# The first pair of MLP-up tiles by eight plain products in the second half of a layer norm, in front of 31 pairs by seven products

## The reference, cut to what matters

```python
h = layer_norm(ALPHA * x + mix, ln1_g, ln1_b)          # (576, 2048)
f = square(relu(einsum('btd,df->btf', h, w_mlp1)))      # w_mlp1 (2048, 8192)
y = layer_norm(ALPHA * h + einsum('btf,fd->btd', f, w_mlp2), ln2_g, ln2_b)
```

## Time and profile before

| | us |
|---|---|
| median of 3 runs | 2711.6 (2711.41 to 2714.79) |
| the profiled execution: its time | 2708.59 |
| its span, first to last instruction | 2706.8 |
| mean granted TensorE clock | 0.986 of full speed |
| PE busy | 2593.7 |
| DVE busy | 2004.7 |
| ACT busy | 1073.2 |

### The profile page before, as it was taken

One profiled execution on the slowest core, in us unless ns is written; L12 is line 12 of the kernel. 1 busy time (PEld: TensorE's weight loads), 2 busy tenths in 40 slices (PEclk: granted clock), 3 DMA queues, 4 the chain that ended last, 5 costly groups with the idle time before them and its releaser, 6 DMA issues.

```text
span 2706.8 us, 51737 instructions
## 1 busy us (share of the span) xinstructions
PE 2593.7 (96%) x20061; PEld 2477.8 (92%) x20061; DVE 2004.7 (74%) x3181; ACT 1073.2 (40%) x1361; POOL 70.3 (3%) x118
## 2 busy tenths in 40 slices
PE   8999999998889999987999999999999999999998
PEld 8999999995657777887999999999999999999997
DVE  5788732326875555689888888888888888888898
ACT  3111111115874444455555555555433333333333
POOL 1000000000000100000000000000000000000001
PEclk9999999998999999998999999999999999999998
DMA  8776643316026775754555555555795556555642
GB/s 260 231 240 207 191 85 79 79 49 237 2 71 213 246 247 176 213 158 138 187 185 187 190 189 188 185 185 185 277 313 181 185 177 211 184 182 180 194 126 86
DMA packets 514888, 480.20 MB, mean 177 GB/s; under 512 B 49276, under 2 KB 465300, under 8 KB 503862
## 3 DMA queue, kind: packets, MB, share of 16 engines
q1 hardware_dynamic: 509722, 411.57, 48.7%
q0 software_dynamic: 4736, 67.18, 6.6%
q10 hardware_dynamic: 332, 0.11, 0.0%
HBM read 387.89 MB, written 99.16 MB: 180 GB/s over the span
## 4 chain that ended last, share of the span: by engine, by line
PE 64%; DVE 6%; ACT 3%; issue 2%; DMA 1%; SPq 1%; DVEq 0%; ACTq 0%
PE ps L2619 50%; PE ps L2535 3%; PE ps L2462 3%; PE ps L2440 2%; PE ps L2330 1%; PE ps L2400 1%; PE ps L2384 1%; PE ps L2320 1%; DVE pS L1574 1%; PE ps L2344 1%; DMA f_b<-f_scratch 1%; PE ps L2416 1%; DVE w_sl L1774 0%; ACT sS L1000 0%; ACT pT L962 0%
## 5 line engine op out<-in xcount | busy, mean ns | idle before, releaser
L1128 ACT ACTIVATE w_sh<-w_s 128x1024 fp32r<-128x1024 f32 (+1 forms) x512 | 473.6, 949 | 783.3 <-PE ps L2619 522.6
L2619 PE MATMUL ps<-f_b,w_sh 128*128 128x288 f32 x3584 | 713.8, 295 | 8.4 <-DMA f_b<-f_scratch 6.0
L1774 DVE TENSOR_TENSOR w_sl<-w_s,w_sh 128x1024 fp32r<-128x1024 f32 (+1 forms) x512 | 554.3, 1088 | 123.9 <-ACT w_sh L1128 123.5
L2619 PEld LDWEIGHTS ps<-f_b,w_sh 128*128 128x128 f32 x3584 | 574.3, 189 | 11.0 <-DMA f_b<-f_scratch 7.0
L2619 PE MATMUL ps<-f_b,w_sl 128*128 128x288 f32 x1792 | 527.1, 294 | 0.0
L2619 PE MATMUL ps<-h_u,w_sh 128*128 128x288 f32 x2560 | 514.3, 296 | 11.4 <-DVE h_u L1909 10.9
L2619 PEld LDWEIGHTS ps<-h_u,w_sh 128*128 128x128 f32 x2560 | 411.1, 189 | 12.9 <-issue 6.8
L2619 PE MATMUL ps<-h_u,w_sl 128*128 128x288 f32 x1280 | 376.6, 294 | 0.0
L2619 PEld LDWEIGHTS ps<-f_b,w_sl 128*128 128x128 f32 x1792 | 338.9, 189 | 0.0
L861 ACT ACTIVATE w_hi<-w_raw 128x2048 fp32r<-128x2048 f32 x61 | 116.9, 1916 | 484.9 <-PE ps L2171 466.3
L2171 PE MATMUL ps<-x_hi,w_hi 128*128 128x288 f32 x1408 | 302.7, 297 | 0.0
(11 more groups left out here) (322 smaller groups left out, 3340.3 us busy)
## 6 DMA issues: line engine op xcount, KB each, us to landing
w_s<-in_w_mlp SPq DMA_DIRECT2D x512, 256.0 KB, 3.7
f_scratch<-f_st SPq DMA_DIRECT2D x32, 2016.0 KB, 9.0
f_b<-f_scratch SPq DMA_DIRECT2D x56, 1152.0 KB, 8.0
w_raw<-in_w_in SPq DMA_DIRECT2D x90, 512.0 KB, 5.1
e_raw<-in_w_out SPq DMA_DIRECT2D x16, 512.0 KB, 4.3
e_raw<-in_w_out SPq DMA_DIRECT2D x64, 128.0 KB, 3.3
wb<-in_cache_win SPq DMA_DIRECT2D x8, 1024.0 KB
w_raw<-in_w_out SPq DMA_DIRECT2D x64, 128.0 KB, 2.9
```

The lines of the kernel that those rows point to most:

```text
L1128: nc.scalar.activation(w_sh[m][:, :, :], blocks, ACT.Copy).then_inc(z_h[m], 1)
L1774: nc.vector.tensor_tensor(w_sl[m][:, :, :], blocks, w_sh[m][:, :, :].bitcast(F32), ALU.subtract).then_inc(z_l[m], 1)
L2619: last = nc.tensor.matmul(ps[:, bank, 0:TH], w[b][:, at_, cols], acts(k, x), start=(start and n == 0), stop=(stop and n == 2), skip_group_ ...
```

## The change

Pair 0 is computed by eight plain products: no block sums, neither of weights nor of activations. Two output tiles, two token halves, 8 steps of two input tiles, three matmuls each: 96 matmuls on the first token half and 96 on the second. Only the other 31 pairs (`KS`) go by seven products, so the loops run one turn fewer, and the structure that pair 0 had in the kernel before (`first_half_pair`, `up_half(0, 1)`) is now pair 1's.

- Weights: ACT copies both units whole (`std_high`, 128x2048), DVE subtracts (`std_low`: unit 0 in one piece, unit 1 in two).
- PE (`std_pair`): products of steps 0 to 3 on the first token half with the mean after the first, the 16 squares, steps 4 to 7 of tile 0, the spread, steps 4 to 7 of tile 1, then the second token half step by step as `h_u` comes.
- Activations: per step j only the two blocks of the second token half are split (`d_high`, `d_low`, 288 elements each); these two loops carry the shifts and scales. The old loop of sums and splits follows them, without shifts and scales; of the split only the wide one of the four sums is left (`h_high`, `h_low`), and the weight splits `low_12`, `low_56`, `low_22` of unit 0 stand behind its step 0.
- Result: ACT takes relu and square from PSUM into `f_std`, SP stores it to `g_scratch`, and when the last `h_low` is done loads it into `f_raw`. From there it goes the way of the others: `f_sums(-1)` is the first thing in DVE's up loop, `f_high(-1)` and `f_low(-1)` come in the second half of the next pair, then `f_store(-1)`.
- SP also issues the two units of the next pair between the units of pair 0 and the stores.

```diff
-NU = 2 * KP
+KS = KP - 1
+NU = 2 * KS
...
+            sp.wait_ge(s_lo, S_MLP + 1)
+            w_blocks(w1_v, 0, STD, 0)
+            sp.wait_ge(s_lo, S_MLP + 3)
+            w_blocks(w1_v, 1, STD, 1)
             for j in range(MP):
...
+            sp.wait_ge(s_acc, 4 + S_MLP)
+            sp.dma_start(g_dram[:, :, :], f_std[:, :, :]).then_inc(y_sv[0], 16)
             up_load(1, 0)
+            sp.wait_ge(y_sv[0], 64)
+            sp.wait_ge(y_sv[1], 80)
+            sp.wait_ge(h_lo_, 4 * MP)
+            sp.dma_start(f_raw[:, 0:4, :], g_dram[:, :, :]).then_inc(y_sv[0], 16)
             up_load(1, 1)
+            f_store(-1)
...
+            std_high(0)
+            std_high(1)
...
             for j in range(MP):
-                h_high(j)
+                d_high(j)
                 if j < MP - 2:
                     shift(2 * j + 4, 1)
                     shift(2 * j + 5, 1)
+            high_14(0, 0, 64)
+            act.wait_ge(s_gemm, 3 + S_MLP)
+            nc.scalar.activation(f_std[:, 0:3, :], banks(1, 3, TH), ACT.Relu)
+            nc.scalar.activation(f_std[:, 3, :], ps[:, 6, 0:TH], ACT.Relu).then_inc(s_acc, 1)
+            act.wait_ge(s_acc, 3 + S_MLP)
+            nc.scalar.activation(f_std[:, :, :], f_std[:, :, :], ACT.Square).then_inc(s_acc, 1)
+            for j in range(MP):
+                h_high(j)
+                if j == 0:
+                    high_12(0, 0)
+                    high_56(0)
+                    high_22(0, 0, 64)
...
-            unit_act(1, 1, 64, lambda: keep_1(0))
-            with act.Fori(1, KP) as i:
+            unit_act(1, 1, 64, lambda: (f_high(-1), keep_1(0)))
+            with act.Fori(1, KS) as i:
...
             for i in range(KT):
-                if i == KT - 1:
-                    sum_1(0, 0, 64)
-                    sum_23(0, 0)
-                    low_14(0, 0)
-                    sum_4(0, 0)
                 residual(S_OUT + i % XR, i, i % XR, 1, i // XR)
                 add_up(S_OUT + i, i, 1)
...
+                if i == KT - 2:
+                    std_low(0, 0, 4)
...
-            low_12(0, 0)
             dve.wait_ge(l_mean, 2)
             for k in range(KT):
                 subtract(k, 1)
-            low_56(0)
-            low_22(0, 0)
+            std_low(1, 0, 2)
             variance(1)
             invert(1)
+            std_low(1, 2, 4)
             dve.wait_ge(l_sd, 4)
             for k in range(4):
                 scale_1(k, 1)
             for j in range(MP):
-                h_sums(j)
                 if j < MP - 2:
                     scale_1(2 * j + 4, 1)
                     scale_1(2 * j + 5, 1)
+                d_low(j)
+            sum_1(0, 0, 64)
+            sum_23(0, 0)
+            low_14(0, 0)
+            for j in range(MP):
+                h_sums(j)
+                if j == 0:
+                    sum_4(0, 0)
                 h_low(j)
+                if j == 0:
+                    low_12(0, 0)
+                    low_56(0)
+                    low_22(0, 0)
...
-            second_half(0, before=False)
-            with dve.Fori(1, KP) as i:
+            f_sums(-1)
+            second_half(0)
+            with dve.Fori(1, KS) as i:
...
+            def std_pair():
+
+                pe.wait_ge(h_lo_, MP)
+                pe.wait_ge(s_lo, S_MLP + 1)
+                for j in range(CK):
+                    for n in range(2):
+                        std_part(n, j, 0)
+                    if j == 0:
+                        mean_half(1)
+                for k in range(KT):
+                    squares_half(k, 1)
+                for n in range(2):
+                    pe.wait_ge(s_lo, S_MLP + 2 + n)
+                    for j in range(CK, MP):
+                        std_part(n, j, 0)
+                    if n == 0:
+                        rep_half(1)
+                for j in range(MP):
+                    pe.wait_ge(h_lo_, MP + 2 * j + 2)
+                    for n in range(2):
+                        last = std_part(n, j, 1)
+                last.then_inc(s_gemm, 1)
...
+            std_pair()
             first_half_pair()
             up_half(0, 1, first=True)
-            with pe.Fori(1, KP) as i:
+            with pe.Fori(1, KS) as i:
```

More of the change, by code:

```diff
@@ L76 @@
 NSTEP = NCH * MP
-NU = 2 * KP
+KS = KP - 1
+NU = 2 * KS
+STD = 1
+Z0 = 64
 WC = CK * P
@@ L1108, in high_a, with std_high @@
                 nc.scalar.activation(h_a[:, j, :, 0, :], blocks_of(j)[:, 0:3:2, :], ACT.Copy).then_inc(h_hi_, 1)
+            def std_high(h):
+                act.wait_ge(z_raw[h], 64)
+                if h:
+                    act.wait_ge(s_gemm, 2 + S_MLP)
+                nc.scalar.activation(d_hi[h][:, :, :], w_s[:, RAW_AT[h]:RAW_AT[h] + 4, :], ACT.Copy).then_inc(s_hi, 1)
             nc.scalar.activation(pt_f[:, 0:1], w_of[:, 0:1], ACT.Sqrt)
@@ L1901, in h_sums, with d_low @@
                 nc.vector.tensor_tensor(raw[:, 4, :], view[:, 2, :], raw[:, 2, :], ALU.subtract).then_inc(h_t3, 1)
+            def d_low(j):
+                for n, (row, b) in enumerate(((0, 3), (3, 1))):
+                    dve.wait_ge(h_hi_, MP + 2 * j + n + 1)
+                    nc.vector.tensor_tensor(h_u[:, j // CK, row, j % CK, 1, :], blocks_of(j)[:, b, :], h_u[:, j // CK, row, j % CK, 0, :].bitcast(F32),
+                                            ALU.subtract).then_inc(h_lo_, 1)
             def h_low(j):
-                dve.wait_ge(h_hi_, MP + 2 * j + 1)
-                nc.vector.tensor_tensor(h_u[:, j // CK, 0, j % CK, 1, :], blocks_of(j)[:, 3, :], h_u[:, j // CK, 0, j % CK, 0, :].bitcast(F32), ALU.subtract).then_inc(h_lo_, 1)
-                dve.wait_ge(h_hi_, MP + 2 * j + 2)
+                dve.wait_ge(h_hi_, 3 * MP + j + 1)
                 dve.wait_ge(h_t3, 3 * j + 3)
@@ L2044, in step_dve @@
                 if opening:
-                    close_7(KP - 1)
+                    close_7(KS - 1)
                 low_12(t, u)
@@ L2104, in _ @@
                 if q == 0:
-                    f_sums(KP - 1)
+                    f_sums(KS - 1)
                 if q == 2:
-                    f_low(KP - 1)
+                    f_low(KS - 1)
             chunk_dve(1, after_first=True)
@@ L2640, in up_product, with std_part @@
                 product(m, UP_BANK[m], h_block(m, h), h == 0, h == 1, ready)
+            def std_part(n, j, half):
+                bank = (2, 3)[n] if half == 0 else (1, 6)[n]
+                h, cols = j // CK, slice(j % CK * P, (j % CK + 1) * P)
+                for a in range(2):
+                    hi, lo = d_hi[h][:, 2 * n + a, cols], d_lo[h][:, 2 * n + a, cols]
+                    x = [h_a[:, j, a, v, :] if half == 0 else h_u[:, h, (3, 0)[a], j % CK, v, :] for v in range(2)]
+                    for m, (w, v) in enumerate(((hi, x[0]), (hi, x[1]), (lo, x[0]))):
+                        last = nc.tensor.matmul(ps[:, bank, 0:TH], w, v, start=(j == 0 and a == 0 and m == 0),
+                                                stop=(j == MP - 1 and a == 1 and m == 2))
+                return last
+            def std_pair():
[4 more added lines that the diff above has]
+                        std_part(n, j, 0)
+                    if j == 0:
+                        mean_half(1)
[12 more added lines that the diff above has]
+                last.then_inc(s_gemm, 1)
             def first_half_pair():
                 pe.wait_ge(s_acc, 2 + S_MLP)
-                mean_half(1)
-                pe.wait_ge(h_lo_, MP)
                 pe.wait_ge(z_l[M1], 1)
                 up_product(M1, 0)
+                pe.wait_ge(s_acc, 3 + S_MLP)
                 pe.wait_ge(z_l[M2], 1)
                 up_product(M2, 0)
-                for k in range(KT):
-                    squares_half(k, 1)
-                rep_half(1)
                 pe.wait_ge(z_l[M3], 1)
@@ L2675, in up_half @@
                     pe.wait_ge(u_v, i)
-                up_product(M5, h, MP + 2 * CK + 2 if first else None)
+                up_product(M5, h, 3 * MP + CK + 1 if first else None)
                 if not first:
```

76 lines of the change are left out of this document (42 added, 34 removed).

## The result

The changed kernel takes 2719.04 us (median of 15 runs, 2715.77 to 2723.18) against 2711.60 us before (15 runs, 2707.96 to 2715.64): ratio 1.0025, 95% interval 1.0018 to 1.0032: **slower**, by a quarter of a per cent. The forecast was 2719.0 in 2712 to 2725.

The account below looks back on a forecast made before the run. The prediction took the norm's second half to be a chain of DVE and ACT, not matmuls. It summed 18.2 + 2.9 + 6.6 - 22.2 = +5.5, with the clock +7.4, on 2711.6 to 2719.0 us; range 2712 to 2725.

Parts of the forecast that it names:

- The frame: Whole change: one loop turn fewer, -22.2 us, against a later first loop turn; everything behind it costed at nothing.
- Step 1: Before the spread: 24 plain matmuls between squares and spread delay all scales and shifts by +1.2 us.
- Step 2: Plain second half: period 1.8 us, three sums now in the open; first `h_sums` starts +18.2 us later.
- PE hides entirely: Plain second half: PE ends near 1229.5; ACT's relu and square end before its first wide copy is due.
- Step 3: Old loop of sums and splits: a chain, no gain from removed work; added unit-0 low parts cost +2.9 us.
- The rival of a shrinking loop: Steps 1 to 7 of the old loop: period could fall to 3.0 us, 8.4 us less, 2710.6; chance 8%.
- Step 4: Last `h_low` to next pair: load, sums and splits in the open, 14.3 us instead of 7.7, +6.6 us.
- Step 5: Clock: PE's 4.5 us wait before the next pair's M1 drops it to half speed, +1.9 us (bounds 0 and 2.3).
- The sum: Whole kernel: +5.5 us, with the clock +7.4 us, giving 2719.0 us on the median, slower.
- about 3 us more: Sign on the profile page: PE busy about 3 us more, from 24 matmuls.

Follow-up runs that it names:

- experiment 1: Changed kernel with DVE making the block sums of step j+1 before the wide subtraction of step j: 2708.99 us, ratio 0.9986.
- experiment 2: Changed kernel with SP loading the plain result as soon as the block sums of step 6 are done: 2717.26 us, ratio 1.0018.
- experiment 5: Changed kernel with the plain result loaded twice in sequence, DVE and ACT waiting for the second load: 2723.03 us, ratio 1.0041.
- experiment 4: Changed kernel with 28 more matmuls, results unread, on PE ahead of the first loop turn: 2719.71 us, ratio 1.0027.
- experiment 8: Changed kernel with sums ahead, early result load, result's way behind the next unit's work, and spread before the 24 plain products: 2704.98 us, ratio 0.9977.
- second pair of profiles: Both kernels run again unedited: before 2712.34 us, ratio 1.0001; changed 2721.18 us, ratio 1.0031.
- experiment 3: Changed kernel with PE spreading the inverse root before the 24 plain products of tile 0's steps 4 to 7: 2722.36 us, ratio 1.0036.
- experiment 6: Changed kernel with the plain result's sums and split put behind the next unit's work, load unmoved: 2717.41 us, ratio 1.0018.
- experiment 7: Kernel before, with block sums of step j+1 ahead of the low parts of step j: 2710.64 us, ratio 0.9998.

## Why the prediction was right

- **The frame** (one pair fewer, -22.2 us, against a later first turn) held: MLP turns of 22.2 us behind the first. From the second turn's M1 to the end the two kernels take 1404.3 and 1406.1 us before, 1407.5 and 1405.1 us after, so single executions differ there by more than the kernels do.
- **Step 1.** The spread was forecast 14.1 us after the projection's last matmul and came at 14.7 (1216.00 - 1201.29), 1.8 later than before and not 1.2. Part of that is the step's own sum: its terms, 0.7 for the squares and 3.2 in place of 2.47, make +1.4 and not +1.2. The rest is size: the squares ended 1.0 us later, and from their end to the spread it took 3.3 us. The variance came some 0.4 us later too, but did not set the place: the inverse root was ready at 1214.46, and PE has no wait between the projection and 1219.9. So the 36 early products were not quite free either, as the step says. The removed unit-0 sums cost nothing: DVE still waits 1.43 us for PE before the last residual.
- **Step 2.** Periods of 1.71 us in place of 1.8 gave back what the spread lost: first `h_sums` at 33.5 us from the projection, forecast 33.8. "PE hides entirely" was not quite right: ACT's relu starts when PE ends, at 33.4 us from the projection and not 32.4 to 32.7, and with the square it held up ACT's first wide copy by some 0.4 us, which step 2 had taken for nothing.
- **Step 3** was the argument that mattered, and held: 4.24 us per step without scales and shifts, read off the last steps of the old loop. The low parts that the step adds took 2.87 us (1239.43 to 1242.30), forecast 2.9. What follows the wide subtraction of step 7 starts 74.5 us from the projection (1275.79 - 1201.29), forecast 74.3 (1250.35 + 18.2 + 2.9 - 1197.14). The rival of a shrinking loop fell, but its price was right: asked for by order (experiment 1), the period went to 2.93 us and the kernel lost 10 us.
- **Step 4.** 14.2 us from the last wide subtraction to the first turn, forecast 14.3; the load 3.5 us, forecast 3.7. Experiments 2 and 5 show from both sides that it sets the path: taken off it gives 2.7 us, doubled it costs 3.5.
- **Step 5.** The clock fell as taken, for 1.7 us (forecast 1.9), in both profiles of the changed kernel and not where the wait was filled (experiments 4 and 8). The premise that waits of about 2 us leave it up held for those two kernels' profiles and not in general (below).
- **The sum** was +7.4 us; the stage shows +7.2 and +7.4, the medians +7.4 and +8.0. That the agreement of the first median is to 0.04 us is chance: its parts missed by up to 0.65 us each, in both directions. One sign was missed: PE busy "about 3 us more" counted the 24 matmuls alone; it was 11.0 us, and 7.6 in the second pair of profiles, 6.6 and 7.2 of them in the stage, where matmuls at the lower clock also count longer.

## What to carry to other kernels

Work that is moved into an engine's idle time must be followed to where its result is needed: here the pair's products were hidden, but its sums, its way through memory and its split landed on DVE's path, and the sums of the next pair lost the work that had covered their chain. When a loop is a chain of two engines, look at a step that already lacks the work you are about to remove: its length tells whether removing it helps. And when a change moves such a loop, reorder it so that the next step's first half stands ahead of this step's second half: that alone was worth 10 us here. With it, the earlier load, the result's way put later and the spread put first, the same change turned from 0.25% slower to 0.23% faster.

## What the runs showed that was not expected

Short waits of PE are followed by a fall of the clock in some executions and not in others. Behind the squares and a wait before the spread it fell in experiment 3 (1.83 us; 0.50 for more than 3 us) and stayed at 1.00 in experiment 8 (1.84 us), with the same work ahead of it. The waits of 1.6 to 2.0 us between the groups of products that go with each wide step, which step 5 took as harmless, were so in both profiles of the kernel before and both of the changed one, but in experiments 2, 3, 6 and 7 the granted clock fell to 0.50 behind one of them (PE next waits 11 to 13 us anyway, and in experiments 2 and 6 the wait ends 69.7 us from the projection as in the changed kernel, so it cost nothing there). So the price of such a wait is better given as a range.

Nor did shortening the wait before the first loop turn help before it was nearly gone. With 4.15 us (the changed kernel, experiment 1), 3.76 (experiment 2), 2.99 (experiment 6), 2.60 (experiment 3) and even 1.80 us behind one of 5.38 (experiment 5) that turn took 23.7 to 23.9 us each time; with 0.43 and 0.38 us (experiments 4 and 8) it took 22.3.
